# Two weight tiles of a unit interleaved element by element, so that a weight load reads its 128 columns 8 bytes apart

## What is computed

```python
h = modulate(rmsnorm(x, norm_mlp[i]), sh2, sc2)
x = x + g2[:, None, :] * squared_relu_mlp(h, w_up[i], w_down[i])
qkv = h @ w_qkv
return o @ w_o
z = h @ w_in[l] + b_in[l]
y_a = u @ conv_w_out[l] + conv_b_out[l]
y_b = (hb * jax.nn.gelu(z_rg, approximate=True)) @ lru_w_out[l]
x = x + m @ w_mix_out[l]
x = x + (jax.nn.silu(h @ ffn_w1[l]) * (h @ ffn_w3[l])) @ ffn_w2[l]
```

## Time and profile before

| | |
|---|---|
| median of two runs | 1012.83 us |
| the profiled execution | 1013.9 us |
| its span, first to last instruction | 1012.1 us |
| TensorE matmuls busy | 977.0 us (97%), 7468 instructions |
| TensorE weight loads busy | 910.6 us (90%), 7468 instructions |
| VectorE busy | 788.2 us (78%) |
| ScalarE busy | 560.6 us (55%) |
| GpSimd busy | 105.1 us (10%) |
| DMA | 222.27 MB, mean 220 GB/s |

### The profile page before, as it was taken

The page is one execution under the profiler, slowest core; times in us unless marked ns, Lnnn a source line. Parts: engine busy times, 40 slices in busy tenths (PEclk is TensorE's granted clock), DMA queues, the critical chain, the costliest instruction groups (busy, mean ns, idle before and its releaser), DMA issues.

```text
span 1012.1 us, 19319 instructions
## 1 busy us (share of the span) xinstructions
PE 977.0 (97%) x7468; PEld 910.6 (90%) x7468; DVE 788.2 (78%) x1370; ACT 560.6 (55%) x922; POOL 105.1 (10%) x134
## 2 busy tenths in 40 slices
PE   4799999999999999999999999999999999999996
PEld 2479998888989899999888999998889999999996
DVE  4757986999777677667876899999998887777554
ACT  3248675444655567776544666677126564444352
POOL 0000000000000000000000000999910000000000
PEclk8799999999999999999999999999999999999998
DMA  9998798887564865554555455453446555555531
GB/s 378 421 419 336 275 378 300 318 325 280 144 203 115 307 239 177 189 186 167 208 179 213 164 193 170 164 208 127 165 139 221 182 187 189 194 179 190 193 116 42
DMA packets 35880, 222.27 MB, mean 220 GB/s; under 512 B 3883, under 2 KB 9180, under 8 KB 9436
## 3 DMA queue, kind: packets, MB, share of 16 engines
q1 hardware_dynamic: 35804, 221.22, 60.6%
HBM read 220.13 MB, written 1.07 MB: 219 GB/s over the span
## 4 chain that ended last, share of the span: by engine, by line
PE 81%; DVE 8%; DMA 4%; ACT 4%; issue 2%; DVEq 0%; SPq 0%; ACTq 0%
PE bank L656 22%; PE bank L645 17%; PE bank L646 16%; PE bank L650 12%; PE bank L982 5%; PE bank L1035 3%; DMA mod_raw<-w_mod 2%; DVE w_lo L1472 2%; PE s_banks L679 1%; ACT w_hi L1109 1%; DVE s_banks L1879 1%; DVE bank L1854 1%; PE s_banks L1035 1%; DMA raw<-weights 1%; DVE ab L1847 1%
## 5 line engine op out<-in xcount | busy, mean ns | idle before, releaser
L1472 DVE TENSOR_TENSOR w_lo<-raw,w_hi 128x1024 fp32r<-128x1024 f32 x284 | 346.3, 1225 | 32.1 <-ACT w_hi L1109 29.7
L1109 ACT ACTIVATE w_hi<-raw 128x1024 fp32r<-128x1024 f32 x284 | 296.1, 1050 | 93.6 <-PE bank L656 89.9
L645 PE MATMUL bank<-xg_hi,w_hi 128*128 128x258 f32 (+1 forms) x1376 | 340.9, 285 | 0.8 <-ACT w_hi L1109 0.5
L646 PE MATMUL bank<-xg_lo,w_hi 128*128 128x258 f32 (+1 forms) x1376 | 336.5, 281 | 0.0
L645 PEld LDWEIGHTS bank<-xg_hi,w_hi 128*128 128x128 f32 x1376 | 259.7, 189 | 5.8 <-issue 4.7
L646 PEld LDWEIGHTS bank<-xg_lo,w_hi 128*128 128x128 f32 x1376 | 260.1, 189 | 0.2
L656 PE MATMUL bank<-xg_hi,w_lo 128*128 128x258 f32 (+1 forms) x1376 | 198.3, 282 | 0.3 <-DVE w_lo L1472 0.3
L656 PEld LDWEIGHTS bank<-xg_hi,w_lo 128*128 128x128 f32 x1376 | 178.5, 189 | 0.8 <-DVE w_lo L1472 0.5
L650 PE MATMUL bank<-hid,w_hi 128*128 128x512 f32 x512 | 127.7, 391 | 0.0
L650 PEld LDWEIGHTS bank<-hid,w_hi 128*128 128x128 f32 x512 | 91.5, 188 | 15.8
L656 PEld LDWEIGHTS bank<-hid,w_lo 128*128 128x128 f32 x512 | 68.5, 188 | 5.3
(11 more groups left out here) (245 smaller groups left out, 1262.0 us busy)
## 6 DMA issues: line engine op xcount, KB each, us to landing
raw<-weights SPq DMA_DIRECT2D x157, 1024.0 KB, 4.9
mod_raw<-w_mod SPq DMA_DIRECT2D x28, 1024.0 KB, 11.4
mod_raw<-w_dots SPq DMA_DIRECT2D x20, 1024.0 KB, 9.6
toep<-bias_by_distance SPq DMA_DIRECT2D x8, 256.0 KB, 5.4
x<-x_in SPq DMA_DIRECT2D x1, 1024.0 KB, 4.9
toep<-bias_by_distance SPq DMA_DIRECT2D x8, 128.0 KB, 3.9
y_out<-yout SPq DMA_DIRECT2D x4, 256.0 KB, 2.4
c_all<-c_row SPq DMA_DIRECT2D x1, 512.0 KB, 14.8
```

Of the source, the lines that this page charges most:

```text
L645: pe.matmul(dst, hi, r_hi, start=start, stop=False, skip_group_check=True)
L646: pe.matmul(dst, hi, r_lo, start=False, stop=False, skip_group_check=True)
L1109: act.activation(pool_w_hi[:, at, :] if name == "pool" and at < 2 else w_hi[:, at % HL, :], raw[:, slot, (at % 2) * UT * P:(at % 2 + 1) * ...
L1472: ve.tensor_tensor(lo, raw[:, slot, (at % 2) * UT * P:(at % 2 + 1) * UT * P], hi.bitcast(F32), ALU.subtract).then_inc(lo_done, 1)
```

## The change

In the layout on the host, `unit` puts two neighbouring tiles (0 and 1, 2 and 3, ...) element by element into one block of 256 elements: column n of the even tile at element 2n, column n of the odd tile at 2n+1. The DMAs, the splits and the order of all instructions are as before. A new helper `tile` gives TensorE the 128 elements of one tile, every second element of its block, and stands where the slices stood.

```diff
+        def tile(unit, s):
+            two = unit[:, (s // 2) * 2 * P:(s // 2 + 1) * 2 * P].rearrange("p (n h) -> p n h", h=2)
+            return two[:, :, s % 2]
...
             def by_high(dst, slot, s, r_hi, r_lo, start, w=(w_hi, w_lo)):
-                hi = w[0][:, slot, s * P:(s + 1) * P]
+                hi = tile(w[0][:, slot, :], s)
...
-                pe.matmul(bank.rearrange("p (a n) -> p a n", a=2), w_hi[:, slot, s * P:(s + 1) * P], both, start=start, stop=False,
+                pe.matmul(bank.rearrange("p (a n) -> p a n", a=2), tile(w_hi[:, slot, :], s), both, start=start, stop=False,
...
             def by_low(dst, slot, s, r_hi, stop, w=(w_hi, w_lo)):
-                lo = w[1][:, slot, s * P:(s + 1) * P]
+                lo = tile(w[1][:, slot, :], s)
...
-                    mm = pe.matmul(out_bank(name, v)[:, 0:SEQ], raw[:, slot, ((at % 2) * UT + k) * P:((at % 2) * UT + k + 1) * P],
+                    mm = pe.matmul(out_bank(name, v)[:, 0:SEQ], tile(raw[:, slot, (at % 2) * UT * P:(at % 2 + 1) * UT * P], k),
...
-                    mm = pe.matmul(out_bank("lru", m)[:, 0:SEQ], raw[:, slot, ((at % 2) * UT + s) * P:((at % 2) * UT + s + 1) * P],
+                    mm = pe.matmul(out_bank("lru", m)[:, 0:SEQ], tile(raw[:, slot, (at % 2) * UT * P:(at % 2 + 1) * UT * P], s),
...
     def unit(tiles):
-        block = np.zeros((P, UT, P), np.float32)
+        block = np.zeros((P, UT // 2, P, 2), np.float32)
         for s, t in enumerate(tiles):
-            block[:, s, :] = t
+            block[:, s // 2, :, s % 2] = t
```

## The result

The changed kernel takes 1029.94 us (1029.78 and 1030.11 in two runs) against 1012.83 before: the ratio is 1.0169, with a 95% interval of 1.0125 to 1.0213. The profiled execution has a span of 1028.3 us, 16.2 us more than before. I had forecast 997 us with a gain by falling into step; 1029.9 is inside my range, but on the other side.

A forecast was written before the change was run, and what follows sets the result against it. TensorE's matmuls, busy 97% of the span, were taken to bound the kernel. Shape gains summed to 19.4 us, less 3 for VectorE, net 16.4: 1013.9 to 997.5, predicted 997 us; range 957 to 1036.

The forecast's parts named there:

- falling into step: Weight load and running matmul both go over 1,024 bytes at equal pace and stop disturbing each other; net 16.4 us, chance 0.46.
- taken off for VectorE: In rx, rg and the gates VectorE would be late next, so 3 us of the summed gain would not arrive.
- the load's share of the loss: In fp32r matmuls, the 3.5 to 4.5 ns lost beside a weight load, taken to go; 19.4 us summed over shapes.
- equal bytes per nanosecond: Load and moving-operand readers, half of 128 bytes apart, would never meet, or meet once, get displaced and stay apart.
- the load keeps its pace: Reading 128 weight columns takes about 102 ns, estimated from loads of 188 and 137 ns; loads still at 188 ns afterwards.
- rival D: Strided loads get slower and 256- and 258-column matmuls wait; over 2% slower, at half speed about 1,500 us; chance 0.10.
- a spare of 11 to 18 ns: Room left by a load's reading of about 102 ns in a matmul spacing of 113 to 120 ns.
- The price of 3.5 to 4.5 ns: Gain per fp32r matmul without the load's disturbance: 4.5 ns at 258 columns, 3.5 ns at 256 in most stages.
- the six places of the earlier trace: Last matmuls before a stall, taken to run without a load: 278 and 279 ns at 258 columns, 276 to 279 at 256.
- C: Rival: strided loads touch twice the memory and disturb running matmuls more; 1030 to 1041 us, chance 0.17.
- is not at its limit: Argument against rival D: the moving operand is read at twice the load's rate, so its path has room.
- took its first half as "free": Cacheline rule for weight loads: an 8-byte step of fp32 has two hits a line and is free; no gain by itself.

The follow-up runs named there:

- f1_stride16: Four tiles interleaved instead of two, so a load reads columns 16 bytes apart, against the changed kernel; 1685.2 us, ratio 1.6652 to the kernel before.

## Why the prediction was wrong

**What held.** TensorE bounds the kernel, and a nanosecond of matmul is nearly always a nanosecond of time. DMAs, splits, VectorE and the native matmuls cost nothing. Stages held by something else swallowed their share, as I had taken off for VectorE: the matmul that begins at 654.8 us before, at the end of rg, begins at 664.7 after, and the one at 679.9, past the gates, at 689.7, so the gates passed on nothing, and the native stage after them neither (419 matmuls in 90 us both times). Summing the shapes: (291 - 289, 285 - 283 and 286 - 283, so 2.3) x 2,112 = 4.9 us, 2 x 2,064 = 4.1 in glu, rx, rg, conv and ffn, 5 x 1,024 = 5.1 in the down projections, about 5 x 528 = 2.6 for f, 4 x 348 = 1.4 for act and about 1 for o, gives 19 us; 16.2 arrived.

**The step that failed** is "I take it that the load's share of the loss goes", the term of 19.4 us. It had two supports. The first, that equal bytes per nanosecond let the readers settle apart, did not come true: no fp32r shape of the earlier trace rows got shorter, and of the three starts tried with a step of 8 bytes none is better than another. What went is the favourable relation that a step of 4 can have (the 276 ns of the earlier trace rows, the 391 of the 512-column matmuls). The second was that the load keeps its pace. I had read its pace as 102 ns from the difference of two durations, and so gave rival D a spare of 11 to 18 ns. A load's period is 112 ns at 4 bytes and 118 at 8. So in a spacing of 113 to 120 ns there were 1 to 8 ns to spare, and the step took 6.

**The price of 3.5 to 4.5 ns** stood on a reading that later runs undo: that the last matmul before a stall shows what a matmul takes without a load. The last one before the stall at 1672.2 us of `f1_stride16` has no other load beside it either:

```profile
L662 PE MATMUL bank<-f_hi,w_lo 128*128 128x256 f32 x1 | 0.4, 397 | 0.0
```

It takes as long as its neighbours, because its own load ended only at 1672.01 us, 190 ns after the matmul's record begins (1671.82). A recorded duration holds the end of the matmul's own load too, so the six places of the earlier trace rows could not tell what a load costs.

**The rivals.** C was nearest in time (1030 to 1041), but doubled lines did not double the 3.5 to 4.5 ns: 2.3 ns came at 258 columns, 1.1 at 320. That something of its kind is a part of the loss is not excluded, for at 258, 320 and 512 columns the load is shorter than the spacing and the step still cost. D was right that the load gets slower and that the native matmuls hide it. It was wrong in the spare and in the 512-column matmuls, which went from 391 to 396. As a plain limit it is also too small: with 118 ns as the least spacing, every shape below 281 ns (118 and the 163) goes to 281. From the earlier trace rows that is about 4 of the 17 us, an estimate: 3 ns for the 512 low products of the down projections, 1 for 688 of the 256-column matmuls, and 1 to 4 for f, act and o. In fact the spacing went past 118, to 120 and 122. D's chance was too low because I argued that the path "is not at its limit" since the moving operand is read at twice the rate. That said nothing about lines: the moving operand gets four elements out of each.

**The rule that I weighed.** The Trainium skill, "SBUF — State Buffer", in the section on the DMA port swizzle: 16-byte cachelines, two hits a line for full bandwidth, a penalty for each crossing. The runs agree with both halves, in numbers: at 16 bytes, one hit a line, the load needs 2.1 times the 112 ns; at 8 bytes, two hits, 118 against 112, full but for 5%. In the prediction I took its first half as "free"; the 5% left the load next to no slack. The rule of the Trainium skill, "TensorE: Matmul & The Clock Gate", section "Step-by-step", that a load takes nothing from a running matmul, agrees with the native matmuls (379 ns with either load) and not with the 512-column ones (391 and 396 ns, their load hidden both times).

**How the 17 us split.** The kernel before at other starts of its weights is 6 to 10 us slower; the changed kernel at the three starts run is 17 to 18 us slower. So the step costs 8 us where the weights start 64 bytes on, and 12 at 32 bytes; the rest of the 17 is the advantage of the start that the kernel before has, which the step destroys. That a load needs 6 ns more is shown by the narrow matmuls. That this alone makes the 8 to 12 us is not shown, and by the estimate above the plain limit is the smaller part. That the same advantage is lost in both cases is argued from the 512-column matmuls, 395 and 396, and not shown. What makes the two readers settle at one spacing or another, and 2 ns above the load's period, stays open.

No version that computes the whole result beats the kernel before.

## What to carry to other kernels

Before a load's access pattern is changed, measure its own period, with matmuls cut so narrow that they can't be the limit; a duration from the trace, or the difference of two, doesn't tell it. With fp32 weights and 256-column matmuls the two were within a few nanoseconds of each other here, so keep the weights' columns next to each other. Only the full fp32 matmuls took a step of 8 bytes for nothing; the 512-column ones lost 5 ns each, and are the cheaper place only for wide steps (23 against some 115 ns at 16 bytes). Where weights and moving operands start within 128 bytes deserves a scan of its own, for it was worth up to 1% here.

## What the runs showed of the hardware

- The period of a load of 128 fp32 columns was 112 ns at 4 bytes from column to column, 118 at 8, 175 at 12 and 234 at 16: for the last three 1.82 to 1.84 ns for each new 16-byte line. At 32 bytes it was 241, 1.88 ns a line.
- The recorded duration of a load at 12 and 16 bytes was 263 and 330 ns, so 88 and 96 more than its period; beside the narrow matmuls, at 4 and 8 bytes, it was 192 and 196, so 80 and 78 more.
- The recorded duration of a matmul held the end of its own load: 397 ns for a last matmul before a stall when the loads took 330.
- The start of the weights within 128 bytes moved the time by 0.6 to 1.0% with neighbouring columns and by nothing outside the intervals with a step of 8 bytes (1.0167 to 1.0176 at 0, 32 and 64 bytes).
- With the step of 8 bytes the spacing of fp32r matmuls went from 117.4 to 120.0 ns at 256 columns, 120.5 to 122.0 at 258 and 146.5 to 147.6 at 320. The 512-column ones went from 391 to 396 ns and full fp32 ones stayed at 379.
